# A hybrid decoder step on one core: which semaphores are cleared between stages

## The chip, the core and the metric

The kernel runs on one core of a Trainium2 chip. The metric is the device time of one execution in microseconds (us), as a median over runs. Five engines work side by side, each on its own list of instructions: TensorE (PE, with its weight loads PEld), VectorE (DVE), ScalarE (ACT), GpSimd (POOL) and SyncE (SP), which here issues most DMAs. They wait for each other only through semaphores, numbered counters that an instruction raises when it is done and another waits on.

## The reference

One decoder layer, on 512 prompt tokens and 8 x 4 sample tokens, model width 1024, all in float32:

```python
h  = x @ w_in
a  = sliding-window attention(rope(q), rope(k), v, sinks)
b  = gated delta rule(silu(conv(qkv)), beta, g), gated RMS norm
x1 = layer_norm(ALPHA * x  + concat(a, b) @ w_o)
x2 = layer_norm(ALPHA * x1 + cross_attention(x1, memory K/V))
x3 = layer_norm(ALPHA * x2 + peer(x2))
```

`peer` scores 128 + 128 keys for each of 8 heads, picks 16 of 128 x 128 experts, and sums gate x gelu(x . u) x v over them. Outputs are x3 and the new caches and states. What is computed is not touched by the change; it concerns only how the stages are kept apart.

## The kernel before

The program is a row of nine stages, each a Python function that writes the instruction lists of all five engines: `phase_project` (h and the convolution), `phase_window` (window attention, and K/V of the memory), `phase_delta` (the delta rule), `phase_mix` (empty), `phase_cross` (w_o, layer norm, cross attention, layer norm), `phase_scores` (the search keys), `phase_hidden` (the u half of the experts), `phase_combine` (the v half and the last norm) and `phase_finish` (empty). Inside a stage the order of each engine's work is written out by hand, and every dependence is a semaphore with a fixed count; the two long stages, hidden and combine, have hardware loops, whose waits are on a register's value. Every stage with work is one `nc.Block`, at whose end all engines meet.

There are two ways to get a semaphore. `c.shared_sem(name)` (L3214) takes one that is held until the whole program is written, and is never cleared by the kernel. `c.sem(name)` (L3204) takes one and notes it in the list `own` of the stage. `run_phases` (L3200) sets up that list, calls the stage, and then:

```python
        nc.clear_and_free_semaphores(own)     # L3207
        nc.all_engine_barrier()               # L3208
```

L3207 sets the stage's semaphores to zero and gives their numbers back, so that the next stage can take them again from zero. It makes instructions on GpSimd alone: for each range of neighbouring numbers one DRAIN and one range clear (in the order's listing the clear is an `ISA` row). With an empty list it makes none. L3208 makes on each engine a DRAIN and a wait for the common release, which GpSimd gives when all have come. It stays for all nine stages.

Before the change, project, window, scores, hidden and combine take nearly all their semaphores from `c.sem`, through `s = c.sem` in the last three (L2267, L2491, L2929). So do delta (L1019), cross (L1621, L1651) and the class `LayerNorm` (L1531), of which both objects, ln1 and ln2, are made in `phase_cross` (L1643, L1644). A few are shared from the start because a load or a result reaches over a stage's end, as `mem_in` (L294), `delta_states_stored` (L1038), `first_u_in` (L2272) or `hidden_stored` (L2493). Steps of one engine on itself are counted in `dve_step` and `act_step` (L3216, L3217), shared too.

Of the kernel before, what the change touches and what calls it, by code (L numbers as in the profile page):

```python
# [27 lines left out]
NT = 5  # L28
# [110 lines left out]
def words(c, at, *shape, rows=P):  # L139

    n = 1
    for s in shape:
        n *= s
    start = max(x for x in c.tensors if x <= at)
    v = c.tensors[start][0:rows, at - start:at - start + n]
    return shaped(v, *shape)
# [9 lines left out]
def cst(c, at, n, rows=P):  # L156
    return c.tensors[0][0:rows, A_CST + at:A_CST + at + n]
# [63 lines left out]
W_RING = 3  # L221
# [41 lines left out]
def phase_project(c):  # L263
# [21 lines left out]
    conv_group = {item[2]: g for g, item in enumerate(plan) if item[0] == "conv" and item[3] == 1}  # L285
    state_group, XG = next(g for g, item in enumerate(plan) if item[0] == "state"), 2 * NT

    ident_in, consts_in, x_in, state_in = c.sem("ident_in"), c.sem("consts_in"), [c.sem(f"x_in{n}") for n in range(NT)], c.sem("conv_state_in")
    piece_in = [c.sem(f"w_in_piece{s}") for s in range(W_RING)]
    w_hi, w_lo, x_lo = c.sem("w_in_high_set"), c.sem("w_in_low_set"), c.sem("proj_x_low_set")  # L290
    group_done, evacuated = c.sem("proj_group_done"), c.sem("proj_evacuated")
    pads, conv_done, sil_done = c.sem("conv_pads_set"), c.sem("conv_chunk_done"), c.sem("conv_silu_done")
    newc_set, rotated = c.sem("new_conv_rows_set"), c.sem("tile_rotated")
    c.mem_in, c.mem_w_in = c.shared_sem("mem_in"), [c.shared_sem(f"mem_weight_in{i}") for i in range(3)]  # L294

    def piece(store, p):
# [233 lines left out]
def phase_window(c):  # L530
# [20 lines left out]
    w_meml = [rounded(c, f"mem_weight_low{i}", a, KD, XD) for i, a in enumerate(W_RAW)]  # L551
    w_memh = [rounded(c, f"mem_weight_high{i}", a, KD, XD) for i, a in enumerate(W_HIGH)]
    mem_in, mem_w_in = c.mem_in, c.mem_w_in
    mem_turned, mem_hi, mem_lo, mem_done, mem_out = (c.sem("mem_" + x) for x in ("turned", "high_set", "low_set", "projected", "projected_out"))
    w_hi, w_lo = c.sem("mem_weight_high_set"), c.sem("mem_weight_low_set")
    mem_stored = [c.sem(f"mem_stored{i}") for i in range(4)]

    hd = words(c, A_HD, NT, 520)
    ss, beta, dg, dtz, alog, dtb = row_scales(c)
    squared = words(c, W_NCO, D)  # L560
    params_in, nco_stored = c.sem("delta_params_in"), c.sem("new_conv_rows_stored")
    small_act, small_dve = c.sem("row_scales_by_act"), c.sem("row_scales_by_dve")

    sink_in, sink_rows_in, keys_in, values_in = c.sem("sinks_in"), c.sem("sink_rows_in"), c.sem("window_cache_keys_in"), c.sem("window_cache_values_in")
    turned, q_out, late_turned, late_out = c.sem("q_turned"), c.sem("q_turned_out"), c.sem("late_turned"), c.sem("late_turned_out")
    scored, masked, expd, ptd, pt_out, av_done, av_out = (
        c.sem(x) for x in ("scores_done", "scores_masked", "exp_done", "probs_turned", "probs_turned_out", "window_av_done",
                           "window_av_out"))
    qm_set, masked_s, divided_s = c.sem("sample_q_set"), c.sem("sample_scores_masked"), c.sem("sample_probs_set")
    stored = c.sem("window_stored")  # L570
    units = [(n, kv) for n in range(4) for kv in range(2)]
    nu = len(units)

# [1686 lines left out]
def phase_scores(c):  # L2260
# [3 lines left out]
    q, key, keyt = words(c, F_Q, 2, 2, QW), c.keys, words(c, F_KEY + 2 * NK, 2, NK)  # L2264
    sc = words(c, F_SC, NT, 16, NK)
    ident = cst(c, K_ID, P)
    s = c.sem  # L2267
    w_in = [s(f"w_pq_in{h}") for h in range(4)]
    keys_turned, keys_out = s("keys_turned"), s("keys_turned_out")
    x_hi, x_lo, w_hi, w_lo = s("x2_high_set"), s("x2_low_set"), s("w_pq_high_set"), s("w_pq_low_set")  # L2270
    q_done, q_out, scored, score_out = s("peer_q_done"), s("peer_q_out"), s("peer_scored"), s("peer_scores_out")
# [193 lines left out]
def phase_hidden(c):  # L2465
# [22 lines left out]
    eid, head_sum, gates_of = small[:, 0:PAIRS], small[:, PAIRS:PAIRS + PH], {4: small[:, 256:384], GT: small[:, 384:512]}  # L2488
    ids, hid_s = words(c, P_IDS, ROWSETS).bitcast(U32), words(c, P_HID, ROWSETS)

    s = c.sem  # L2491
    u_in, gates_stored = ([s(f"{x}{i}") for i in range(2)] for x in ("expert_u_in", "gates_stored"))
    hid_stored = c.hid_stored = [c.shared_sem(f"hidden_stored{i}") for i in range(2)]  # L2493
    c.first_v, c.first_gated = c.shared_sem("first_expert_v_in"), c.shared_sem("first_gates_in")
# [5 lines left out]
    turned, ut_kept, ut_low, hid_done, gelu_done = (s("expert_" + x) for x in ("u_turned", "u_kept", "u_low_set", "hidden_done", "gelu_done"))  # L2500
# [413 lines left out]
def phase_combine(c):  # L2914
# [11 lines left out]
    gain, bias = cst(c, K_SWA, D), words(c, O_BIAS, D)  # L2926
    stats, mean, root, eps = words(c, O_ST, NT, 12), words(c, O_ST + NT * 12, NT, 2), words(c, O_ST + NT * 14, NT), words(c, O_ST + NT * 15, 1)
    ident = cst(c, K_ID, P)
    s = c.sem  # L2929
    g_in, h_in = ([s(f"{x}_in{i}") for i in range(2)] for x in ("gates", "hidden"))  # L2930
    v_in = [[s(f"expert_v_in{i}{e}") for e in range(2)] for i in range(2)]
    v_hi, v_lo, gated_set, g_hi, g_lo, out_done, tile_out = (s("expert_" + x) for x in (
# [1 line left out]
    x_hi, x_lo, x_added, one_set, eps_set = (s(x) for x in ("x3_high_set", "x3_low_set", "x3_added", "identity_rounded", "eps_set"))  # L2934
    row_in, row_used = [s(f"value_row_in{i}") for i in range(V_RING)], s("value_row_used")
    norm_in, quads_added = s("last_gain_and_bias_in"), s("sample_quads_added")
    var_set, std_set, y_set, stored = (s("last_" + x) for x in ("variance_set", "deviation_set", "half_tile_set", "y_stored"))
# [273 lines left out]
def hymba_step(nc, dram):  # L3211
    with ExitStack() as ctx:
# [18 lines left out]
        with ExitStack() as layer:  # L3231
            memory(layer, "layer", A_FREE, ARENA)
            run_phases(c, (phase_project, phase_window, phase_delta, phase_mix, phase_cross))
        with ExitStack() as search:
            c.xr = high_low(search, "x2_high_low", 2 * KD * TOK)
            memory(search, "scores", F_SC, F_SC_END)
            with ExitStack() as queries:
                c.wr = high_low(queries, "w_pq_high_low", 4 * KD * 2 * NK)
                memory(queries, "queries", F_SC_END, F_END)
                run_phases(c, (phase_scores,))  # L3240
            with ExitStack() as experts:
                c.utr = high_low(experts, "u_high_low", 4 * D)
                c.hot = high_low(experts, "one_hots", 2 * 3 * 4 * P)
                c.gate_hi = high_low(experts, "gates_high", TOK)
                memory(experts, "experts", F_SC_END, H_END)
                run_phases(c, (phase_hidden,))
        with ExitStack() as outputs:
            c.vr = high_low(outputs, "v_high_low", 4 * GB * D)
            c.gr = high_low(outputs, "gated_high_low", 4 * GB * TOK)
            memory(outputs, "outputs", A_FREE, O_END)  # L3250
            run_phases(c, (phase_combine,))
# [23 lines left out]
```

## Time and profile before

| | us |
|---|---|
| median of 3 runs | 2130.9 |
| lowest and highest run | 2126.84 and 2132.81 |
| the profiled execution | 2129.74 |
| its span, first to last instruction | 2127.9 |
| stage project | 0 to 174.5 |
| window | 174.5 to 282.5 |
| delta | 282.5 to 437.7 |
| cross | 437.7 to 699.9 |
| scores | 699.9 to 818.5 |
| hidden | 818.5 to 1564.3 |
| combine | 1564.3 to 2127.9 |

The stages follow each other with no overlap of their instructions. In the profile, busy time of an engine counts only its computing instructions (and GpSimd's indirect DMAs); drains, waits and semaphore clears are listed under the engine's name with a q, as POOLq, and are seen only when their line is asked for. `PEclk` is the clock granted to TensorE, 1.00 being full speed; a DMA share of 1 means that all 16 DMA engines of the core are busy.

### The profile page before, as it was taken

How to read it: one execution, taken by the hardware profiler on the slowest of the kernel's cores; microseconds unless marked ns; L12 is line 12 of the kernel's file. 1: busy time of each engine (PE TensorE's matmuls, PEld its weight loads, DVE VectorE, ACT ScalarE, POOL GpSimd, SP SyncE). 2: the span in 40 equal slices, each digit the busy share in tenths (PEclk: the TensorE clock that was granted, in tenths of full speed). 3: DMA queues.
4: the chain of work that ended last, by engine and by line, in shares of the span. 5: the costliest groups of instructions: out<-in, count | busy, mean ns of one | idle time of the engine just before them, and what ended most of it. 6: DMA issues, size and time to landing. Idle time of an engine off the chain costs nothing. (4 is left out here: it accounts for less than half of the span.)

```text
span 2127.9 us, 33947 instructions
## 1 busy us (share of the span) xinstructions
PE 2032.2 (96%) x12943; PEld 1856.7 (87%) x12943; DVE 1620.7 (76%) x3030; ACT 792.9 (37%) x1311; POOL 536.1 (25%) x334
## 2 busy tenths in 40 slices
PE   7999989889999899999999999999989999999998
PEld 7998879878856899999999999999978787787786
DVE  5735756565254326999999799999969888889898
ACT  4335453342241322323244444444433333333332
POOL 0000010000000000212112055555536555665530
PEclk9999989999999999999999999999999999999999
DMA  5224210061451403677667479998899999999993
GB/s 170 80 84 130 81 52 1 21 222 40 178 198 43 159 1 105 246 250 268 230 215 268 146 281 339 344 340 338 334 363 387 386 387 387 383 383 384 380 376 112
DMA packets 223184, 483.75 MB, mean 227 GB/s; under 512 B 11983, under 2 KB 137167, under 8 KB 221414
## 3 DMA queue, kind: packets, MB, share of 16 engines
q1 hardware_dynamic: 176998, 314.56, 41.5%
q0 software_dynamic: 46080, 167.79, 21.6%
q8 instruction: 65, 1.06, 0.2%
q14 instruction: 41, 0.34, 0.0%
HBM read 423.29 MB, written 58.36 MB: 226 GB/s over the span
## 5 line engine op out<-in xcount | busy, mean ns | idle before, releaser
L2990 PE MATMUL ps<-v_high_low,gated_high_low 128*128 128x512 f32 x2304 | 534.7, 393 | 22.5 <-ACT gated_high_low L3058 18.1
L2990 PEld LDWEIGHTS ps<-v_high_low,gated_high_low 128*128 128x128 f32 x2304 | 434.1, 189 | 122.9 <-ACT v_high_low L3056 20.4
L2594 PE MATMUL ps<-x_high_low,u_high_low 128*128 128x384 f32 x1024 | 356.4, 348 | 0.0
L2595 PE MATMUL ps<-x_high_low,u_high_low 128*128 128x384 f32 x1024 | 345.6, 337 | 0.0
L3082 POOL DMA_INDIRECT outputs<-peer_v,kept x138 | 245.5, 1779 | 180.8 <-DVE kept L3099 148.1
L2711 POOL DMA_INDIRECT scores<-peer_u,kept x64 | 93.9, 1468 | 732.5 <-DVE kept L2831 555.4
L2669 ACT ACTIVATE kept<-ps 128x384 f32<-128x384 f32 x128 | 62.9, 491 | 405.6 <-PE ps L2599 399.2
L2599 PE MATMUL ps<-x_high_low,u_high_low 128*128 128x384 f32 x1024 | 204.7, 341 | 0.0
L2595 PEld LDWEIGHTS ps<-x_high_low,u_high_low 128*128 128x128 f32 x1024 | 193.4, 189 | 0.0
L2594 PEld LDWEIGHTS ps<-x_high_low,u_high_low 128*128 128x128 f32 x1024 | 193.0, 188 | 0.0
L3162 DVE TENSOR_TENSOR v_high_low<-raw_v,v_high_low 128x1024 fp32r<-128x1024 f32 x120 | 146.2, 1218 | 53.4 <-ACT v_high_low L3056 53.4
L2599 PEld LDWEIGHTS ps<-x_high_low,u_high_low 128*128 128x128 f32 x1024 | 178.4, 188 | 0.0
L3099 DVE SCALAR_TENSOR_TENSOR kept<-outputs,kept 128x1024 f32<-128x1024 f32 x136 | 174.0, 1279 | 4.7 <-DMA outputs<-peer_v,kept 0.9
L2724 DVE TENSOR_TENSOR u_high_low<-ps,u_high_low 128x1024 fp32r<-128x1024 f32 x128 | 156.1, 1219 | 27.7 <-ACT u_high_low L2660 27.1
L3056 ACT CAST v_high_low<-raw_v 128x1024 fp32r<-128x1024 f32 x120 | 125.9, 1049 | 104.2 <-DMA raw_v<-peer_v 102.8
L3058 ACT CAST gated_high_low<-outputs 128x384 fp32r<-128x384 f32 x128 | 65.7, 513 | 240.5 <-DVE outputs L3156 237.2
L2660 ACT CAST u_high_low<-ps 128x1024 fp32r<-128x1024 f32 x128 | 133.6, 1044 | 37.4 <-PE ps L2585 33.0
L2711 POOL DMA_INDIRECT experts<-peer_u,kept x64 | 93.1, 1455 | 151.0 <-DVE experts L2732 144.0
L2585 PE MATMUL ps<-kept,experts 128*128 128x128 f32 x1008 | 130.6, 273 | 0.0
L2585 PEld LDWEIGHTS ps<-kept,experts 128*128 128x128 f32 x1008 | 116.4, 141 | 3.0 <-issue 0.2
L2680 ACT COPY scores<-ps 128x512 f32<-128x512 f32 x96 | 97.8, 1133 | 0.0
L1520 POOL TENSOR_TENSOR layer<-layer,kept 128x512 f32<-128x512 f32 (+1 forms) x5 | 6.0, 1191 | 308.1 <-DVE layer L1415 308.1
(471 smaller groups left out, 4144.8 us busy)
## 6 DMA issues: line engine op xcount, KB each, us to landing
experts<-peer_u SPq DMA_DIRECT2D x63, 1024.0 KB
raw_v<-peer_v SPq DMA_DIRECT2D x60, 1024.0 KB
hidden<-kept SPq DMA_DIRECT2D x64, 384.0 KB
gates<-scores SPq DMA_DIRECT2D x12, 2048.0 KB
first_hidden<-hidden SPq DMA_DIRECT2D x16, 768.0 KB, 17.9
outputs<-gates SPq DMA_DIRECT2D x16, 768.0 KB
outputs<-hidden SPq DMA_DIRECT2D x16, 768.0 KB
first_gates<-gates SPq DMA_DIRECT2D x15, 768.0 KB
```

Source lines behind the costliest of these rows:

```text
L2585: ins = pe.transpose(bank(c, 4 * b, D)[:, P * k:P * k + P], block_u[:, P * k:P * k + P], ident)
L2594: pe.matmul(o, utr[:, b, HI, k], xr[:, HI, k, 0:DN], start=(k == 0), stop=False)
L2595: pe.matmul(o, utr[:, b, HI, k], xr[:, LO, k, 0:DN], start=False, stop=False)
L2599: ins = pe.matmul(o, utr[:, b, LO, k], xr[:, HI, k, 0:DN], start=False, stop=(k == KD - 1))
L2660: act.copy(utr[:, b, HI], bank(c, 4 * b, D).rearrange("p (k a) -> p k a", k=KD)).then_inc(ut_kept, 1)
L2711: pool.indirect_dma_start(out=ring[i], out_offset=None, in_=d.peer_u[0], in_offset=bass.IndirectOffsetOnAxis(ap=ids[:, no:no + 1], axis=0) ...
L2724: v.tensor_tensor(utr[:, n % 2, LO], bank(c, 4 * (n % 2), D).rearrange("p (k a) -> p k a", k=KD), plain(utr[:, n % 2, HI]), ALU.subtract). ...
L2990: ins = pe.matmul(bank(c, 2 * t + h), gr[:, slot, x, DN * b + P * t:DN * b + P * t + P], vr[:, slot, y, D * b + 512 * h:D * b + 512 * h + ...
L3056: act.copy(vr[:, slot, HI, D * b:D * b + D], raw).then_inc(v_hi, 1)
L3082: pool.indirect_dma_start(out=ring[i], out_offset=None, in_=d.peer_v[0], in_offset=bass.IndirectOffsetOnAxis(ap=ids[:, no:no + 1], axis=0) ...
L3099: ins = v.scalar_tensor_tensor(into, row, g, into, ALU.mult, ALU.add)
L3162: v.tensor_tensor(vr[:, slot, LO, D * b:D * b + D], raw, plain(vr[:, slot, HI, D * b:D * b + D]), ALU.subtract).then_inc(v_lo, 1)
```

## The change

In project, window, scores, hidden and combine every `c.sem` becomes `c.shared_sem`. These semaphores are no longer in `own`, so L3207 does not clear them, and their numbers are not used again; each later stage takes numbers of its own. L3207, L3208, `LayerNorm`, `phase_delta` and `phase_cross` are as before. In words the change is that the semaphores of five stages and of both layer norms live to the program's end, and only those of the delta rule and of cross attention are cleared between stages; of the layer norms, the diff has nothing.

```diff
-    ident_in, consts_in, x_in, state_in = c.sem("ident_in"), c.sem("consts_in"), [c.sem(f"x_in{n}") for n in range(NT)], c.sem("conv_state_in")
+    ident_in, consts_in, x_in, state_in = c.shared_sem("ident_in"), c.shared_sem("consts_in"), [c.shared_sem(f"x_in{n}") for n in range(NT)], c.shared_sem("conv_state_in")
...
-    newc_set, rotated = c.sem("new_conv_rows_set"), c.sem("tile_rotated")
+    newc_set, rotated = c.shared_sem("new_conv_rows_set"), c.shared_sem("tile_rotated")
...
@@ phase_window
-    params_in, nco_stored = c.sem("delta_params_in"), c.sem("new_conv_rows_stored")
+    params_in, nco_stored = c.shared_sem("delta_params_in"), c.shared_sem("new_conv_rows_stored")
...
-    stored = c.sem("window_stored")
+    stored = c.shared_sem("window_stored")
...
@@ phase_scores, phase_hidden, phase_combine (one line in each)
-    s = c.sem
+    s = c.shared_sem
```

What it moves is seen on GpSimd. Its list from the program's start to the end of the cross and scores stages (`L1514` opens its part of delta, `L2703` its part of hidden; rows with - are of before, with + of the change):

```order
 L3263 MEMSET const-bfloat16-1.0 128x1
 L3263 MEMSET const-uint8-127 128x1
-L3207 ISA x3
 L1514 UNCONDITIONAL_BRANCH
 L1520 ISA
...
 L1522 TENSOR_TENSOR layer<-kept,layer 32x128
 L1050 UNCONDITIONAL_BRANCH
-L3207 ISA x9
+L3207 ISA x5
 L2703 UNCONDITIONAL_BRANCH
```

The three clears after project and window are gone, and of the nine after delta, cross and scores five are left. The same list from the end of hidden (`L2517`) through combine (`L3073` opens it) to the end of the program:

```order
 L2711 DMA kept<-peer_u,kept 128x1024
 L2517 UNCONDITIONAL_BRANCH
-L3207 ISA x5
 L3073 UNCONDITIONAL_BRANCH
 L3082 DMA outputs<-peer_v,kept 128x1024 x3
...
 L2954 UNCONDITIONAL_BRANCH
-L3207 ISA x5
```

Both groups of five are gone. On the other four engines every instruction keeps its place; only the numbers of the semaphores that they raise and wait on differ.

## Rows read from the trace of the kernel before

**Rows 1.** the page, part 4: the chain that ended last, share of the span by line
```profile
DMA raw_v<-peer_v 7%; SPq L2968 4%; DVE kept L3099 4%; PE ps L2990 2%; DVE v_high_low L3162 2%; DVE outputs L3156 1%; DMA outputs<-gates 1%; ACT v_high_low L3056 1%; DMA outputs<-peer_v,kept 1%; SPq L2966 0%; DVE gated_high_low L3167 0%; PE
```

**Rows 2.** stretches: start:end us, length, busy us of each engine, PEclk, DMA share, GB/s
```profile
818.50:1564.30 745.80, 739.15 (x4875) 735.52 (x4875) 705.60 (x1682) 300.77 (x375) 234.03 (x160) 1.00 0.76 275
1564.30:2127.90 563.60, 538.73 (x2320) 436.74 (x2320) 489.46 (x586) 195.01 (x266) 290.07 (x160) 0.98 0.97 357
```

**Rows 3.** instructions of L3207 over the span: ns min/median/max, first to last start
```profile
L3207 POOLq DRAIN  x22: 42/68/98, 174.2 to 2127.0; - x22
L3207 POOLq EVENT_SEMAPHORE_RANGE_CLEAR  x22: 45/80/175, 174.3 to 2127.1; - x22
```

**Rows 4.** instructions of L3207, then of L3208, from 436 to 439 us
```profile
L3207 POOLq DRAIN  x3: 53/77/95, 436.7 to 437.3; - x3
...
L3208 POOLq DRAIN  x2: 40/40/40, 437.5 to 437.7; - x2
L3208 PEldq EVENT_SEMAPHORE  x2: 51/51/51, 437.7 to 438.0; - x2
```

**Rows 5.** the same two lines, from 173 to 175.5, then 281 to 284 us
```profile
L3207 POOLq DRAIN  x1: 98/98/98, 174.2 to 174.2; - x1
...
L3208 PEldq EVENT_SEMAPHORE  x1: 51/51/51, 174.7 to 174.7; - x1
...
L3207 POOLq DRAIN  x2: 70/79/88, 281.9 to 282.2; - x2
...
L3208 PEldq EVENT_SEMAPHORE  x1: 51/51/51, 282.7 to 282.7; - x1
```

**Rows 6.** the same, from 698.5 to 701, 817 to 820, 1563 to 1566 us
```profile
L3207 POOLq DRAIN  x4: 67/86/95, 698.7 to 699.4; - x4
...
L3208 PEldq EVENT_SEMAPHORE  x1: 51/51/51, 700.0 to 700.0; - x1
...
L3207 POOLq DRAIN  x2: 49/60/71, 817.5 to 817.7; - x2
L3207 POOLq EVENT_SEMAPHORE_RANGE_CLEAR  x2: 45/68/92, 817.6 to 818.1; - x2
...
L3208 PEldq EVENT_SEMAPHORE  x1: 51/51/51, 818.5 to 818.5; - x1
...
L3207 POOLq DRAIN  x5: 42/58/81, 1563.2 to 1563.8; - x5
...
L3208 PEldq EVENT_SEMAPHORE  x1: 51/51/51, 1564.3 to 1564.3; - x1
```

**Rows 7.** the same, from 2126 to 2128 us (combine and the empty last stage)
```profile
L3207 POOLq DRAIN  x5: 55/58/87, 2126.4 to 2127.0; - x5
...
L3208 PEldq EVENT_SEMAPHORE  x2: 51/51/51, 2127.5 to 2127.9; - x2
```

**Rows 8.** stretches around boundaries, columns as in rows 2
```profile
173.00:175.50 2.50, 1.18 (x12) 0.93 (x9) 0.02 (x1) 1.09 (x2) 0.00 (x0) 1.00 0.00 0
436.00:439.00 3.00, 0.86 (x4) 0.89 (x5) 0.39 (x1) 0.30 (x1) 0.00 (x0) 0.50 0.92 291
819.80:823.20 3.40, 3.40 (x15) 3.38 (x13) 3.37 (x14) 2.91 (x3) 0.00 (x0) 0.50 0.90 337
823.20:826.60 3.40, 3.40 (x22) 3.37 (x22) 3.40 (x22) 0.51 (x2) 0.00 (x0) 1.00 0.90 224
```

**Rows 9.** timeline: start us, us, engine, line, operation, [idle before <-releaser]
```profile
174.82 0.63 PE L634 MATMUL ps<-kept,layer 128*128 128x128 f32 x4 [1.32 <-PEq L3208]
...
818.61 2.55 PE L2585 MATMUL ps<-kept,first_u 128*128 128x128 f32 x16 [2.02 <-PEq L3208]
...
1566.09 8.74 SPq L2968 DMA_DIRECT2D outputs<-hidden  x1
```

**Rows 10.** the chain in order of time: start us, us, what
```profile
1728.46 12.56 DMA raw_v<-peer_v
...
1862.65 15.98 DMA raw_v<-peer_v
```

More of the change, by code:

```diff
@@ L286, in phase_project @@
     state_group, XG = next(g for g, item in enumerate(plan) if item[0] == "state"), 2 * NT
-    ident_in, consts_in, x_in, state_in = c.sem("ident_in"), c.sem("consts_in"), [c.sem(f"x_in{n}") for n in range(NT)], c.sem("conv_state_in")
[L289 to L292, printed above, removed]
-    newc_set, rotated = c.sem("new_conv_rows_set"), c.sem("tile_rotated")
+    ident_in, consts_in, x_in, state_in = c.shared_sem("ident_in"), c.shared_sem("consts_in"), [c.shared_sem(f"x_in{n}") for n in range(NT)], c.shared_sem("conv_state_in")
+    piece_in = [c.shared_sem(f"w_in_piece{s}") for s in range(W_RING)]
+    w_hi, w_lo, x_lo = c.shared_sem("w_in_high_set"), c.shared_sem("w_in_low_set"), c.shared_sem("proj_x_low_set")
+    group_done, evacuated = c.shared_sem("proj_group_done"), c.shared_sem("proj_evacuated")
+    pads, conv_done, sil_done = c.shared_sem("conv_pads_set"), c.shared_sem("conv_chunk_done"), c.shared_sem("conv_silu_done")
+    newc_set, rotated = c.shared_sem("new_conv_rows_set"), c.shared_sem("tile_rotated")
     c.mem_in, c.mem_w_in = c.shared_sem("mem_in"), [c.shared_sem(f"mem_weight_in{i}") for i in range(3)]
@@ L553, in phase_window @@
     mem_in, mem_w_in = c.mem_in, c.mem_w_in
-    mem_turned, mem_hi, mem_lo, mem_done, mem_out = (c.sem("mem_" + x) for x in ("turned", "high_set", "low_set", "projected", "projected_out"))
-    w_hi, w_lo = c.sem("mem_weight_high_set"), c.sem("mem_weight_low_set")
-    mem_stored = [c.sem(f"mem_stored{i}") for i in range(4)]
+    mem_turned, mem_hi, mem_lo, mem_done, mem_out = (c.shared_sem("mem_" + x) for x in ("turned", "high_set", "low_set", "projected", "projected_out"))
+    w_hi, w_lo = c.shared_sem("mem_weight_high_set"), c.shared_sem("mem_weight_low_set")
+    mem_stored = [c.shared_sem(f"mem_stored{i}") for i in range(4)]
     hd = words(c, A_HD, NT, 520)
@@ L560, in phase_window @@
     squared = words(c, W_NCO, D)
-    params_in, nco_stored = c.sem("delta_params_in"), c.sem("new_conv_rows_stored")
-    small_act, small_dve = c.sem("row_scales_by_act"), c.sem("row_scales_by_dve")
-    sink_in, sink_rows_in, keys_in, values_in = c.sem("sinks_in"), c.sem("sink_rows_in"), c.sem("window_cache_keys_in"), c.sem("window_cache_values_in")
-    turned, q_out, late_turned, late_out = c.sem("q_turned"), c.sem("q_turned_out"), c.sem("late_turned"), c.sem("late_turned_out")
+    params_in, nco_stored = c.shared_sem("delta_params_in"), c.shared_sem("new_conv_rows_stored")
+    small_act, small_dve = c.shared_sem("row_scales_by_act"), c.shared_sem("row_scales_by_dve")
+    sink_in, sink_rows_in, keys_in, values_in = c.shared_sem("sinks_in"), c.shared_sem("sink_rows_in"), c.shared_sem("window_cache_keys_in"), c.shared_sem("window_cache_values_in")
+    turned, q_out, late_turned, late_out = c.shared_sem("q_turned"), c.shared_sem("q_turned_out"), c.shared_sem("late_turned"), c.shared_sem("late_turned_out")
     scored, masked, expd, ptd, pt_out, av_done, av_out = (
-        c.sem(x) for x in ("scores_done", "scores_masked", "exp_done", "probs_turned", "probs_turned_out", "window_av_done",
+        c.shared_sem(x) for x in ("scores_done", "scores_masked", "exp_done", "probs_turned", "probs_turned_out", "window_av_done",
                            "window_av_out"))
-    qm_set, masked_s, divided_s = c.sem("sample_q_set"), c.sem("sample_scores_masked"), c.sem("sample_probs_set")
-    stored = c.sem("window_stored")
+    qm_set, masked_s, divided_s = c.shared_sem("sample_q_set"), c.shared_sem("sample_scores_masked"), c.shared_sem("sample_probs_set")
+    stored = c.shared_sem("window_stored")
     units = [(n, kv) for n in range(4) for kv in range(2)]
@@ L2489, in phase_hidden @@
     ids, hid_s = words(c, P_IDS, ROWSETS).bitcast(U32), words(c, P_HID, ROWSETS)
-    s = c.sem
+    s = c.shared_sem
     u_in, gates_stored = ([s(f"{x}{i}") for i in range(2)] for x in ("expert_u_in", "gates_stored"))
@@ L2928, in phase_combine @@
     ident = cst(c, K_ID, P)
-    s = c.sem
+    s = c.shared_sem
     g_in, h_in = ([s(f"{x}_in{i}") for i in range(2)] for x in ("gates", "hidden"))
```

## The prediction

> **What bounds the kernel now.** I read the page first. Of the span of 2127.9 us, the chain that ended last runs through the loads of `peer_v`, VectorE and SyncE's queue in the last long stage [rows 1]. Nothing in these rows names a semaphore clear. Then the table by stage: the expert stage is filled by TensorE (739.15 of 745.8 us), the combining stage by its transfers (DMA share 0.97) [rows 2]. The change touches neither, so the question is only what stands between the stages. For that I asked for the instructions of L3207, the call that clears: 22 pairs of a DRAIN and a range clear, all on GpSimd, medians 68 and 80 ns [rows 3]. They are not counted as busy, so the engine table says nothing of them. What they cost must be read from the other engines: how long after a stage's end they are let go.
>
> **How a boundary runs.** At the end of a stage, all engines meet once (the Block's own barrier). Then GpSimd clears; the four others go straight to the barrier of L3208 and stand there. GpSimd joins only after its last clear, and then releases all. Nothing hides the clears, because every engine is stopped. The cost of a boundary is thus from GpSimd's first DRAIN of L3207 to TensorE's EVENT_SEMAPHORE of L3208. The program has one boundary without any clear, that of the empty `phase_mix`: there GpSimd's DRAIN of L3208 is at 437.7 and TensorE's release at 438.0, so a bare barrier takes 0.3 us [rows 4]. That is what remains where all clears go.
>
> **The sum, boundary by boundary.** Starts are printed to 0.1 us, so each difference may be off by as much, and the sum by some 0.3.
> - After project: 174.2 to 174.7 is 0.5 us with one pair, less 0.3: **0.2 us** goes [rows 5].
> - After window: 281.9 to 282.7 is 0.8 with two pairs: **0.5** [rows 5].
> - After delta: 436.7 to 437.7 is 1.0 with three pairs, so a pair costs (1.0 - 0.3)/3 = 0.23 [rows 4]. Its semaphores are still cleared. The order on GpSimd shows 9 clears of delta, cross and scores becoming 5, and scores keeps none. So 7 of delta and cross become 5: shared semaphores no longer lie scattered between the cleared numbers, and there are fewer ranges. I put one pair to each of the two stages: **0.2** here.
> - After cross: 698.7 to 700.0 is 1.3 with four pairs, a pair 0.25: **0.3** [rows 6].
> - After scores: 817.5 to 818.5 is 1.0 with two pairs: **0.7** [rows 6].
> - After hidden: 1563.2 to 1564.3 is 1.1 with five: **0.8** [rows 6].
> - After combine: 2126.4 to 2127.5 is 1.1 with five: **0.8** [rows 7]. This one is at the very end of the program, where nothing can take it back.
>
> That makes 3.5 us for 17 pairs removed, 0.2 us each. The other engines' instruction counts do not change; the waits on their instructions carry other semaphore numbers, which I cost at nothing, since the same events release them: 0.1 us after TensorE is released at 174.7 it runs its first matmul [rows 5, 9], whatever the number is called.
>
> The price of a pair has two bounds. The cheapest is the marginal pair at the end, 0.8/5 = 0.16 us, which gives 17 x 0.16 = 2.7. The dearest are the two after scores, 0.7/2 = 0.35, which gives 6.0. I take the sum by boundaries, 3.5, since each term has its own row. As a further floor only the 0.8 us at the end is kept, if each earlier stage waited for something that does not move with it.
>
> One term is doubtful. After scores, the second DRAIN takes at most 71 ns from 817.7 and its clear begins only at 818.1 [rows 6]: some 0.4 us in which GpSimd runs nothing. I count it as gained. If the gap belongs to the place in the instruction stream and not to the clear, it appears at another GpSimd instruction, and the gain is 3.1. The Trainium skill, Runtime: NRT & Kernel Launch, Instruction fetch mechanics, says that an engine's instructions come in blocks by the engine's own queue, and that crossing a block is mostly but not wholly hidden; by that rule the gap stays in the program and the sum is 3.1. No row here shows which instruction a block begins with. The same page (The launch sequence) has the runtime zero the user semaphores around the kernel whatever the kernel leaves in them; by that, the time outside the span does not grow. The profiled execution took 2129.74 us with a span of 2127.9, so 1.8 us lie outside it, and I leave them as they are.
>
> **Does a gain at a boundary last?** After project TensorE starts 0.1 us behind the release, after 1.32 us of idle time; after scores it starts at 818.61, 0.1 us behind the release at 818.5, after 2.02 us of idle time, and is busy from there on [rows 5, 6, 9]. The loads and gathers of a stage are issued by SyncE and GpSimd, which are released with the rest, so they move together with the work that uses them. So I let all 3.5 us through.
>
> Against the profiled execution: 2129.74 - 3.5 = 2126.2. It lay 1.2 us under the median of the three runs shown, 2130.9; so for the median, **2130.9 - 3.5 = 2127.4 us**, 0.16% less. The three runs spread from 2126.84 to 2132.81, more than the whole effect; about 0.3% (6.4 us) is what a measurement of this kernel can tell from no change.
>
> **Rivals.**
> - *The gain is swallowed* (chance 0.1). Loads in flight over a boundary land when they land. For it: across the boundary after delta the DMA share is 0.92 from 436 to 439 us, so early weights could be the next wait. Against it: TensorE starts that stage with the release, only the 0.2 us of that boundary hangs on it, and around the boundary after project the DMA share is 0.00 [rows 8]. For more to be lost, later stages would have to wait for loads issued a stage earlier. Kept: 0.8 to 2 us, time 2129 to 2130.
> - *The clock gives more* (0.13). After scores the granted clock is 0.50 from 819.8 to 823.2, and in that time 15 matmuls run where 22 run in the next 3.4 us at 1.00 [rows 8] (0.50 and 1.00 are 1.2 and 2.4 GHz): 3.4 x (1 - 15/22) = 1.1 us lost, and it came after the idle time of 2.02 us [rows 9], which the change cuts to 1.3. Around the boundary after project, with 1.32 us of idle time, the clock stays at 1.00 [rows 8]. If the fall does not come, 1.1 us more is gained, and a second one elsewhere may shorten too (0.50 around the boundary after delta [rows 8]): 3.5 + 1.1 to 2.2, time 2125 to 2126. With a measurement a little low this reads as faster by over 0.3%.
> - *The combining stage settles worse* (0.04): slower. Its transfers fill it, and its start is crowded: SyncE's first load of `hidden` is stuck 8.74 us in issuing [rows 9]. The release comes 0.8 us earlier, and the balance of GpSimd's gathers and SyncE's loads may fall otherwise. The chain waits 12 times for `raw_v`, mostly near 12.56 us, at the longest 15.98 [rows 10]. Each one that goes from the one to the other costs 3.4 us, so one pays back the gain and three give 10.3 - 3.5 = 6.8 us more than now, slower by over 0.3%: 2137.7. Against it: all loads and gathers of the stage start from the same release, so their distances stay.
> - *The change does not do all that its words say.* They name both layer norms, but `LayerNorm` (L1531) still takes its semaphores from `c.sem`, and both are made in `phase_cross`, so they are cleared with cross. It is in my count already (7 pairs to 5, not fewer), and worth about one pair, 0.2 us.
>
> **The numbers.** The forecast has 0.73, the swallowed gain 0.1, the clock 0.13, the slower case 0.04. From the spread of the runs a fifth or so of the first and third cases together would read as faster by over 0.3%: faster 0.16, same 0.80, slower 0.04. The range: dearest pair and the clock give 6.0 + 1.1 = 7.1 us, 2123.8, and 2.3 below that for the scatter of the runs, 2121.5; at the other end 0.8 us gained is 2130.1, and the highest run lay 1.9 above its median: 2132.0. The slower case lies outside.
>
> **What would show it.** After: 5 pairs of L3207 in place of 22, two after delta and three after cross; TensorE's release 0.3 us after the first L3208 DRAIN of GpSimd at the other boundaries; the lengths of the seven stages between releases unchanged but for a us or two; no 0.50 just after the start of the expert stage, or still one; time outside the span still 1.8. I am wrong if the pairs gone do not shift the release, if a stage between two releases is several us longer or shorter, or if GpSimd's 0.4 us gap turns up where another engine waits for it.

## The result, and the profile after

| | kernel before | changed kernel |
|---|---|---|
| median | 2129.62 us (20 runs) | 2133.26 us (20 runs) |
| lowest and highest | 2125.51 to 2133.68 | 2129.56 to 2138.32 |
| ratio, 95% interval | | 1.0021 (1.0014 to 1.0029) |
| span of the profiled execution | 2127.9 | 2130.4 |

The change made the kernel slower, by 0.21% or some 4.5 us by the ratio (3.6 between the medians). That is under the 0.3% that I had called same, but the interval leaves the sign clear, and I had forecast 3.5 us less.

The clears went as counted. Of the 22 pairs on L3207 [rows 3] five are left, two after delta and three after cross. First the lines for the whole span in the changed kernel's profile, then those around delta's and cross's ends (instructions of a line: ns min/median/max, first to last start):

```profile
L3207 POOLq DRAIN  x5: 64/90/128, 432.1 to 696.7; - x5
L3207 POOLq EVENT_SEMAPHORE_RANGE_CLEAR  x5: 45/175/291, 432.3 to 696.9; - x5
```

```profile
L3207 POOLq DRAIN  x2: 64/96/128, 432.1 to 432.6; - x2
...
L3207 POOLq DRAIN  x3: 67/90/116, 696.1 to 696.7; - x3
...
L3208 PEldq EVENT_SEMAPHORE  x1: 51/51/51, 697.3 to 697.3; - x1
```

After delta the longer of the two clears that are left takes 291 ns, where the longest of before took 175 [rows 3]. I put that down to the same semaphores lying in fewer, longer ranges; no view shows how long a range is. From GpSimd's first DRAIN to the release the boundary after cross takes 696.1 to 697.3, 1.2 us, in place of 1.3 [rows 6]. The boundary after delta takes 0.9 (432.1 to 433.0) in place of 1.0 [rows 4]. The fewer ranges brought 0.1 us at each of the two, not 0.2 and 0.3.

Where nothing is cleared any more and GpSimd has done no gathers, the boundary is the bare barrier of 0.3 us. The lines of L3208 after project (GpSimd's DRAIN, TensorE's release), after window and after scores (release alone; the Blocks ended 0.3 us earlier):

```profile
L3208 POOLq DRAIN  x1: 41/41/41, 173.0 to 173.0; - x1
L3208 PEldq EVENT_SEMAPHORE  x1: 51/51/51, 173.3 to 173.3; - x1
...
L3208 PEldq EVENT_SEMAPHORE  x1: 51/51/51, 280.6 to 280.6; - x1
...
L3208 PEldq EVENT_SEMAPHORE  x1: 51/51/51, 815.6 to 815.6; - x1
```

After scores that is 0.3 for 1.0 us [rows 6], after project 0.3 for 0.5 and after window 0.3 for 0.8 [rows 5]. So far the sum holds. The loss is in the other two boundaries. L3208 after hidden, and after combine:

```profile
L3208 POOLq DRAIN  x1: 4224/4224/4224, 1559.1 to 1559.1; - x1
L3208 PEldq EVENT_SEMAPHORE  x1: 51/51/51, 1563.5 to 1563.5; - x1
...
L3208 POOLq DRAIN  x1: 4457/4457/4457, 2125.4 to 2125.4; - x1
...
L3208 PEldq EVENT_SEMAPHORE  x2: 51/51/51, 2130.0 to 2130.3; - x2
```

GpSimd's own DRAIN takes **4224 ns** after hidden and **4457 ns** after combine. In the kernel before, the same instruction took 40 ns there, behind five clears (L3208 from 1563 to 1566 us, then from 2126 to 2128, where the empty last stage has the second):

```profile
L3208 POOLq DRAIN  x1: 40/40/40, 1564.1 to 1564.1; - x1
...
L3208 POOLq DRAIN  x2: 40/40/40, 2127.3 to 2127.6; - x2
```

In the changed kernel all engines stand there until it is done: the release after hidden comes at 1563.5, 4.4 us after the DRAIN's start, instead of 1.1 us [rows 6]; that after combine 4.6 us after it, instead of 1.1 [rows 7]. These are the two stages in which GpSimd issues gathers (indirect DMAs, L2711 and L3082), 160 in each, and it had long stopped: its last gather of the combining stage starts at 2051.20, 74 us ahead of that DRAIN (timeline, as in rows 9):

```profile
2051.20 1.01 POOL L3082 DMA_INDIRECT kept<-peer_v,kept  x1 [2.30 <-DVE kept L3099]
```

The transfers had landed too. By the DMA view, the queue that carries the gathers (`software_dynamic`) has no packet from 1552.9 to the DRAIN at 1559.1, and none from 2058.2 to the one at 2125.4: the last gather was done 6 us ahead of the one DRAIN and 67 us ahead of the other.

To see whether anything else had moved, here are four of the seven stages by themselves, without the boundaries, and the sum over all seven (columns as in rows 2). Before, then after:

```profile
282.70:436.70 154.00, 132.08 (x1232) 125.57 (x1232) 103.14 (x201) 73.77 (x210) 11.76 (x10) 0.92 0.11 32
438.00:698.70 260.70, 243.41 (x1509) 188.91 (x1509) 133.82 (x188) 74.66 (x147) 0.00 (x0) 0.98 0.37 132
818.50:1563.20 744.70, 739.15 (x4875) 735.52 (x4875) 705.60 (x1682) 300.77 (x375) 234.03 (x160) 1.00 0.76 275
1564.30:2126.40 562.10, 538.73 (x2320) 436.74 (x2320) 489.46 (x586) 195.01 (x266) 290.07 (x160) 0.99 0.98 358
sum 2120.40, PE 2032.22 PEld 1856.72 DVE 1620.69 ACT 792.93 POOL 536.07; mean PE 290.32 PEld 265.25 DVE 231.53 ACT 113.28 POOL 76.58
```

```profile
280.60:432.10 151.50, 130.31 (x1232) 123.51 (x1232) 103.15 (x201) 73.83 (x210) 11.77 (x10) 0.93 0.11 33
433.30:696.10 262.80, 246.50 (x1509) 191.01 (x1509) 133.84 (x188) 75.10 (x147) 0.00 (x0) 0.97 0.37 131
815.60:1559.10 743.50, 737.83 (x4875) 734.00 (x4875) 705.54 (x1682) 300.84 (x375) 234.47 (x160) 1.00 0.77 276
1563.50:2125.40 561.90, 537.15 (x2320) 435.45 (x2320) 489.23 (x586) 194.98 (x266) 298.90 (x160) 0.99 0.98 358
sum 2117.70, PE 2031.16 PEld 1854.44 DVE 1620.43 ACT 793.88 POOL 545.34; mean PE 290.17 PEld 264.92 DVE 231.49 ACT 113.41 POOL 77.91
```

What is left of the span when the stages are taken out is 2127.9 - 2120.4 = 7.5 us before and 2130.4 - 2117.7 = 12.7 us after: **5.2 us more at the boundaries**. Without the two DRAINs (4.224 + 4.457, less the 0.08 that two short ones take) it would be 4.1 us, 3.4 less than before: that is the forecast's 3.5. The stages differ by -2.5 us (delta), +2.1 (cross), -1.2 (hidden) and -1.2 (project, from its length of 174.2 and 173.0) in these two executions, 2.7 us less in all. Such differences need no cause in the change: over the profiles below, delta alone took from 148.69 to 156.30 us.

### The profile page after: what moved, and what is told of

It reads as the page before. It is cut to its first block and busy times, and to the rows that moved or that the text cites. A ratio compares the mean times of both kernels' runs of the same rounds, so it can differ in the third digit from the quotient of the medians.

```text
span 2130.4 us, 33913 instructions
## 1 busy us (share of the span) xinstructions
PE 2031.2 (95%) x12943; PEld 1854.4 (87%) x12943; DVE 1620.4 (76%) x3030; ACT 793.9 (37%) x1311; POOL 545.3 (26%) x334
## 5 line engine op out<-in xcount | busy, mean ns | idle before, releaser
L3082 POOL DMA_INDIRECT outputs<-peer_v,kept x138 | 256.8, 1861 | 175.5 <-DVE kept L3099 139.6
L2711 POOL DMA_INDIRECT scores<-peer_u,kept x64 | 94.1, 1470 | 730.4 <-DVE kept L2831 553.6
L2711 POOL DMA_INDIRECT experts<-peer_u,kept x64 | 93.2, 1457 | 150.8 <-DVE experts L2732 143.8
```

Of the source, the lines that this page charges most:

```text
L2711: pool.indirect_dma_start(out=ring[i], out_offset=None, in_=d.peer_u[0], in_offset=bass.IndirectOffsetOnAxis(ap=ids[:, no:no + 1], axis=0) ...
L3082: pool.indirect_dma_start(out=ring[i], out_offset=None, in_=d.peer_v[0], in_offset=bass.IndirectOffsetOnAxis(ap=ids[:, no:no + 1], axis=0) ...
```

## The experiments

The question was why a DRAIN of 40 ns became one of 4.2 us, and whether that alone is the result. Theory A: the first plain DRAIN (one of a barrier) on GpSimd behind gathers costs, the DRAIN that comes with a semaphore clear does not, and it spares the one behind it. Theory B: the cost comes from semaphores left uncleared. Further ones are in the expectations. The first four kernels ran on one chip with the kernel before at a median of 2129.1 us.

### One unused semaphore, cleared after each of the two stages

```diff
         phase(c)
+        if phase in (phase_hidden, phase_combine):
+            c.sem(f"spare_{phase.__name__}")
```

> The changed kernel, but the expert stage and the combining stage each take one unused semaphore from c.sem, so that L3207 makes one DRAIN and one range clear there. In the changed kernel's profile GpSimd's DRAIN of L3208 after these two stages took 4224 and 4457 ns (it took 40 ns before). Theory A (the first plain DRAIN after gathers costs 4.2 to 4.5 us; the DRAIN of a clear does not, and settles it): both barriers take 0.5 us instead of 4.35 and 4.58, the span is 7.9 us shorter than the changed kernel's, about 2125.5 us in time, ratio 0.998 to the kernel before. Theory B (the 4 us come from the gathers' own semaphores being left uncleared): both DRAINs of L3208 stay at 4.2 to 4.5 us, time 2133, ratio 1.002. Theory C (the DRAIN of a clear only starts the work, which then must run out): the DRAIN of L3208 behind the single clear takes about 4 us, ratio 1.002.

Measured: 2124.93 us (12 runs), ratio **0.9987** (0.9977 to 0.9997), which is 0.13% faster than the kernel before. The lines of the clear (here L3209) and of the barrier (here L3210) after hidden:

```profile
L3209 POOLq DRAIN  x1: 53/53/53, 1559.9 to 1559.9; - x1
L3209 POOLq EVENT_SEMAPHORE_RANGE_CLEAR  x1: 44/44/44, 1560.0 to 1560.0; - x1
...
L3210 POOLq DRAIN  x1: 40/40/40, 1560.1 to 1560.1; - x1
L3210 PEldq EVENT_SEMAPHORE  x1: 51/51/51, 1560.3 to 1560.3; - x1
```

The clear's DRAIN after combine:

```profile
L3209 POOLq DRAIN  x1: 58/58/58, 2121.7 to 2121.7; - x1
```

One clear of one semaphore that nothing ever raised, 53 + 44 ns, and the barrier's DRAIN is 40 ns again. The boundary takes 0.4 us from the first DRAIN to the release. Theory B falls, since all the gathers' semaphores are still uncleared, and so does C: the work is not just started and waited for later. The span is 2122.4 us, 8.0 less than the changed kernel's; by the two ratios to the kernel before, the gain is 0.34%, some 7 us. The two DRAINs had taken 8.7.

### A plain DRAIN early, hidden behind the other engines

```diff
                 pool.indirect_dma_start(...).then_inc(row_in[i], 16)
+            pool.drain()
```

Behind the gather loop, in hidden and in combine.

> The changed kernel with a plain DRAIN of GpSimd right behind its last gather of the expert stage and of the combining stage, where it has more than ten us left until the stage ends. Theory A (a fixed cost of the first plain DRAIN after gathers, paid by GpSimd alone): these new DRAINs take 4 us or more each, hidden behind the other engines, and the DRAINs of L3208 take 0.04 us; the barriers take 0.25 us each, the time falls by 8.4 us to about 2125, ratio 0.998. Theory B (uncleared semaphores are looked through at every plain DRAIN): both the new DRAINs and those of L3208 take 4 us, ratio 1.002. Theory D (the DRAIN waits for transfers of the gathers still under way): the new DRAIN is as long as the last gather's transfer, and L3208's is short; but then the changed kernel's could not have been 4 us long, 13 us or more behind the last gather.

Measured: 2125.48 us (12 runs), ratio **0.9981** (0.9971 to 0.9991). The new DRAINs in hidden and in combine, and all nine of the barriers:

```profile
L2713 POOLq DRAIN  x1: 11545/11545/11545, 1542.8 to 1542.8; - x1
...
L3085 POOLq DRAIN  x1: 10572/10572/10572, 2046.3 to 2046.3; - x1
...
L3210 POOLq DRAIN  x9: 34/40/41, 172.5 to 2120.1; - x9
```

The DRAINs take 11.5 and 10.6 us where they stand. The last transfers are still under way: the last packet of the gathers' queue lands at 1551.7 and at 2054.1, 2.6 and 2.8 us ahead of the DRAIN's end. Nobody waits for them. No barrier's DRAIN is longer than 41 ns. So a plain DRAIN spares the next one too, and what it costs depends on where it stands. Here waiting for transfers and the cost of the changed kernel are added up and can't be told apart; that a DRAIN waits for transfers alone is excluded by the changed kernel, where they had landed 6 and 67 us before.

### No barrier, or one without DRAINs, where nothing was cleared

```diff
-        nc.clear_and_free_semaphores(own)
-        nc.all_engine_barrier()
+        if own:
+            nc.clear_and_free_semaphores(own)
+            nc.all_engine_barrier()
```

> The changed kernel without L3208 where nothing was cleared (project, window, the empty mix, scores, hidden, combine, the empty finish): the meeting at the end of each Block is the only one left there. Theory A: all that these seven barriers took goes, 0.25 us five times and 4.35 and 4.58 us, together 10.2 us: time about 2123, ratio 0.997. If the 4 us are work that GpSimd owes after its gathers whatever comes next, they turn up elsewhere, at its first instruction of the combining stage (hidden there, nothing waits within 4 us but the gathers) or beyond the program's last instruction (time minus span grows from 1.8 to 6 us): ratio 1.000.

Measured: 2125.38 us (12 runs), ratio **0.9987** (0.9977 to 0.9996). And with the barrier kept, but of semaphores alone:

```diff
-        nc.all_engine_barrier()
+        nc.all_engine_barrier(sem_only=not own)
```

> The changed kernel with the barrier of L3208 kept everywhere, but made of semaphores alone, with no DRAIN on any engine, where nothing was cleared. Theory A: the two long barriers fall from 4.35 and 4.58 to 0.2 us, time 8.6 us or more less, about 2124.5, ratio 0.998. If the 4 us belong to the meeting and not to the DRAIN, they stay: ratio 1.002.

Measured: 2127.04 us (12 runs), ratio **0.9988** (0.9977 to 0.9998). The cost belongs to the DRAIN and not to the meeting, and it is not owed: with no DRAIN of GpSimd at all behind the gathers, in either kernel, the loss is gone, and the time outside the span of the profiled execution is 1.8 us in both, as before. The first of the two should have gained 2.3 us more than the kernel with the unused semaphore (10.2 against 7.9 us expected); that can't be seen in the intervals. In its profile delta took 156.30 us and combine 563.03, more than in the profiles of the kernel before, of the changed kernel and of the other three. That is one execution, the third slowest of its twelve, so it does not explain the median; where the missing gain went stays open.

### The changed kernel again

> The changed kernel once more, on the same chip as the next three and with a second profile. If the long DRAINs of L3208 belong to the program, they are there again, 4.2 and 4.5 us within 0.1, the time is near 2133 and the ratio to the kernel before near 1.002. If they were a chance of one execution, they are short and the time of the changed kernel has another cause. The lengths of the stages, which in its first profile were 2.5 us less for delta and 2.1 us more for cross than in the profile of before, show by how much they scatter.

Measured: 2135.2 us (7 runs), ratio **1.0027** (1.0016 to 1.0038) to the kernel before at 2130.8 us on this chip. All DRAINs of L3208:

```profile
L3208 POOLq DRAIN  x9: 34/40/4457, 174.3 to 2132.4; - x9
```

The longest is 4457 ns, to the nanosecond that of the first profile; the one after hidden took 4224 again. So this is no scatter of transfers or of the clock. The stages do scatter: the DRAIN after project starts at 174.3 against 173.0 us, and hidden takes 745.5 (814.0 to 1559.5) against 743.5 for the same program.

### The kernel before, with a barrier ahead of its clears

```diff
+        if phase in (phase_hidden, phase_combine):
+            nc.all_engine_barrier()
         nc.clear_and_free_semaphores(own)
         nc.all_engine_barrier()
```

> The kernel before, all its semaphores cleared as before, with one more barrier (plain DRAINs) ahead of the clears after the expert stage and after the combining stage. Theory A (the first plain DRAIN after gathers costs, whatever is cleared later): the new barriers' DRAINs take 4.2 and 4.5 us, the clears and the old barriers stay as they were; the span grows by 2 x 0.3 + 8.4 = 9 us, time about 2138, ratio 1.004. Theory B (it is the semaphores left over from earlier stages that make a DRAIN long; here none is left but the shared ones): all DRAINs short, two barriers of 0.3 us more, ratio 1.000.

Measured: 2140.01 us (7 runs), ratio **1.0044** (1.0027 to 1.0061). After hidden, the new barrier (L3208: DRAIN and release), the clears (L3209) and the old barrier (L3210), then the new one's DRAIN after combine:

```profile
L3208 POOLq DRAIN  x1: 4218/4218/4218, 1564.6 to 1564.6; - x1
L3208 PEldq EVENT_SEMAPHORE  x1: 51/51/51, 1569.0 to 1569.0; - x1
...
L3209 POOLq DRAIN  x5: 47/60/81, 1569.0 to 1569.7; - x5
...
L3210 POOLq DRAIN  x1: 40/40/40, 1569.9 to 1569.9; - x1
...
L3208 POOLq DRAIN  x1: 4465/4465/4465, 2131.7 to 2131.7; - x1
```

All semaphores are cleared as before, and yet the plain DRAIN that now comes first takes 4218 and 4465 ns. Order decides, not which semaphores live on. This is the loss of the change, brought about in the kernel before with no semaphore's life altered.

### A MEMSET of GpSimd in between

```diff
         nc.clear_and_free_semaphores(own)
+        if phase in (phase_hidden, phase_combine):
+            nc.gpsimd.memset(c.scratch[:, :], 0.0)
         nc.all_engine_barrier()
```

> The changed kernel with one small MEMSET on GpSimd (128x1) between the end of the Block and the barrier, after the expert stage and after the combining stage. If any instruction of the GpSimd engine after the gathers settles them, the DRAINs of L3208 fall to about 0.05 us. If only the DRAIN of a clear does, they stay at 4.2 and 4.5 us. If the MEMSET pays in the DRAIN's place, the release is as late as before.

Measured: 2131.7 us in a single run, which says nothing of the time; its trace is what counts here. The memset (L3209) and the barrier's DRAINs after it (L3210), after hidden and after combine:

```profile
L3209 POOL MEMSET scratch<- x2: 99/99/99, 1558.5 to 2124.8; 128x1 f32 x2
...
L3210 POOLq DRAIN  x1: 4350/4350/4350, 1558.5 to 1558.5; - x1
...
L3210 POOLq DRAIN  x1: 4584/4584/4584, 2124.8 to 2124.8; - x1
```

This compute instruction settles nothing; the DRAIN is 0.13 us longer than in the changed kernel (4350 for 4224, 4584 for 4457), about the 99 ns of the memset.

### By what the cost goes

```diff
                 pool.indirect_dma_start(...).then_inc(row_in[i], 16)
+                if no == ROWSETS // 2 - 1:
+                    pool.drain()
```

In both stages, so that 80 of the 160 gathers are left behind it.

> The changed kernel with a plain DRAIN of GpSimd in the middle of its gathers, behind half of them, in the expert stage and in the combining stage. If the cost of the first plain DRAIN is by the number of gathers since the last one, the DRAINs of L3208 halve to some 2.1 and 2.2 us; if it is fixed, they stay at 4.2 and 4.5 us and the middle ones are as long or longer, since transfers are under way there.

The DRAINs of the barrier (here L3212) after hidden and after combine:

```profile
L3212 POOLq DRAIN  x1: 6587/6587/6587, 1566.5 to 1566.5; - x1
...
L3212 POOLq DRAIN  x1: 6577/6577/6577, 2136.2 to 2136.2; - x1
```

Neither of the two expectations: fewer gathers since the last DRAIN, and the next takes *longer*, 6.58 us for 4.2 and 4.5. The single run took 2145.15 us, its span 2143.3; the middle DRAINs themselves took 16.3 and 13.5 us among running gathers. The last gathers had landed as far back as before (hidden: no packet of theirs from 1560.3 to the DRAIN at 1566.5), so 6587 ns after hidden and 6577 after combine, some 6 and 67 us behind the last landing, show that it is the number of gathers that counts and not how long ago they ended. A cost per gather that is forgotten from time to time would do this, which the next two kernels test. They move the DRAIN:

```diff
+                if no == ROWSETS - 21:
+                    pool.drain()
```

with 21 in hidden and 41 in combine for the first, 121 and 11 for the second.

> The changed kernel with a plain DRAIN of GpSimd ahead of its last 20 gathers of the expert stage and ahead of its last 40 of the combining stage. A DRAIN of L3208 took 4.2 and 4.5 us behind 160 gathers since the last plain DRAIN, and 6.6 us behind 80. Theory E (the DRAIN goes through the gathers since the last one that are still on its list, 6.58/80 = 0.082 us each; behind 160 most are off the list already, since the list is short): behind 20 it takes 1.6 us, behind 40 3.3 us. Theory F (fixed, and more where a DRAIN stood among the gathers): both take 6.6 us.

> The same with the DRAIN ahead of the last 120 gathers of the expert stage and ahead of the last 10 of the combining stage. Theory E: 0.8 us behind 10; behind 120 either up to 9.8 us, if the list holds as many, or less than 6.6, if it has been shortened on the way. Theory F: both 6.6 us.

DRAINs of L3212 after hidden and after combine, first kernel (20 and 40 gathers):

```profile
L3212 POOLq DRAIN  x1: 1687/1687/1687, 1563.9 to 1563.9; - x1
...
L3212 POOLq DRAIN  x1: 3311/3311/3311, 2127.4 to 2127.4; - x1
```

Second kernel (120 and 10 gathers):

```profile
L3212 POOLq DRAIN  x1: 952/952/952, 1561.6 to 1561.6; - x1
...
L3212 POOLq DRAIN  x1: 861/861/861, 2124.8 to 2124.8; - x1
```

Their times were 2133.09 and 2127.96 us, a single run each; the moved DRAINs themselves took from 7.8 to 11.1 us, with transfers under way. Theory F falls. In a table, gathers since the last plain DRAIN against the barrier's DRAIN:

| gathers | 10 | 20 | 40 | 80 | 120 | 160 |
|---|---|---|---|---|---|---|
| us | 0.861 | 1.687 | 3.311 | 6.58 | 0.952 | 4.218 to 4.465 |

From 10 to 80 it is a line: (6.587 - 0.861)/70 = 0.082 us for each gather, and 0.04 us besides. Behind 120, in hidden, it is what 11 cost by this line; behind 160 what 51 cost in hidden and 54 in combine. So after some 109 gathers in hidden (120 - 11 and 160 - 51) and 106 in combine GpSimd's count starts anew. That is worked out from three points, and the two of hidden lie apart by the same price, (4.224 - 0.952)/40 = 0.082 us. It fits a list of gathers which a plain DRAIN goes through one by one, finished or not, and which empties itself when it is full; the runs show the sawtooth, not the list.

## Why the prediction was wrong

- **What a boundary costs, and that nothing hides it.** Right. The bare barrier is 0.3 us in all places where the forecast used it without gathers, and all that GpSimd adds comes out in the release.
- **17 pairs less, 5 left, two after delta and three after cross.** Right. Their sum was 3.5 us; measured at the boundaries, with the two long DRAINs taken out, 3.4. With one spare clear in each of the two stages 0.13% is won (0.03 to 0.23%), 2.8 us by the ratio, which agrees with that price within a wide interval (0.6 to 4.9 us). Two terms were too large: delta's and cross's, 0.2 and 0.3 us, measured 0.1 each, since the ranges that are left take longer.
- **The step that failed** is the one that reads best: "That is what remains where all clears go", the 0.3 us taken from the boundary of the empty `phase_mix` [rows 4] and used for hidden and combine too. Mix has no gathers before it. The DRAIN of L3208 was short after hidden and combine only because five clears stood ahead of it. In the sum these two terms were gains of 0.8 us each; they are losses of 4.4 - 1.1 = 3.3 and 4.6 - 1.1 = 3.5 us. The other five, forecast at 1.9 us, measured 0.2 + 0.5 + 0.1 + 0.1 + 0.7 = 1.6: 3.3 + 3.5 - 1.6 = 5.2 us lost by starts read to 0.1 us, 5.2 by the stages taken out of the span, 4.5 in the time by the ratio. By the prediction's own sign, a release 0.3 us after the DRAIN of L3208 wherever nothing is cleared, it was wrong at these two boundaries and right at the others.
- **The rivals.** My slower rival had the wrong place (the loads of the combining stage, which took 561.9 us after 562.1) and a chance of 0.04. None of the four rivals had the mechanism: removing an instruction changes what the next one costs. The row to doubt it by was there: two boundaries of nine follow gathers, and neither was ever seen without a clear.
- **The gap of 0.4 us after scores** was gained with the clears; 0.3 us is left there. In the kernel before with a barrier more, whose program is the same up to there, it is back at the same place, the second DRAIN at most 71 ns from 819.8, its clear at 820.3:

```profile
L3209 POOLq DRAIN  x2: 49/60/71, 819.7 to 819.8; - x2
L3209 POOLq EVENT_SEMAPHORE_RANGE_CLEAR  x2: 45/68/92, 819.8 to 820.3; - x2
```

  So the gap is no chance of one execution. Whether it belongs to that pair or to the place in the instruction stream is not settled, and the DMA view speaks for the place. One of its two queues of the kind `instruction`, q14, has a transfer 0.6 to 0.7 us behind the late clear in both programs, at 818.8 us in the kernel before and at 820.9 with the barrier more. In the changed kernel q14 has none from 814 to 820 us; one comes at 821.7, 6 us into the expert stage. The view for 818 to 820, then 820 to 822 with the barrier more, then 820 to 822 in the changed kernel (packets, MB, share of 16 engines):

```profile
q14 instruction: 1, 0.01, 1.0%
...
q14 instruction: 1, 0.01, 1.7%
...
q14 instruction: 1, 0.01, 2.1%
```

  The view does not name the engine that the instructions are for; a list of GpSimd that is shorter by the removed pairs would move its transfers in this way. The doubt that I took from the Trainium skill (Runtime: NRT & Kernel Launch, Instruction fetch mechanics), by which the gap would stay in the program, is thus not answered. At the boundaries it cost nothing, since none of the changed kernel shows a gap and the 0.4 us were gained there; inside a stage no view used here would show it. That page has the runtime zero the semaphores in any case (The launch sequence); the time outside the span, 1.8 us before and after, agrees.
- **The clock.** In the changed kernel no stretch of 0.50 follows scores, as the rival asked; nor does one in the nine other profiles of kernels with the change, where TensorE is idle for 1.01 to 1.43 us there. But the kernel before with a barrier more has the full 2.02 us of idle time there and no fall either (timeline of TensorE, then stretches as in rows 2):

```profile
820.76 1.94 PE L2585 MATMUL ps<-kept,first_u 128*128 128x128 f32 x16 [2.02 <-PEq L3210]
...
819.60:823.00 3.40, 2.01 (x17) 1.80 (x17) 2.24 (x12) 1.13 (x2) 0.00 (x0) 1.00 0.34 86
823.00:826.00 3.00, 3.00 (x17) 3.00 (x18) 2.97 (x14) 2.08 (x2) 0.00 (x0) 1.00 1.05 362
```

  So of the two executions with 2.02 us of idle time one had the fall and one had not: that idle time does not bring it by itself. Whether the shorter one keeps it away stays open, and with it whether the 1.1 us are the change's to give in some executions; the medians show nothing of it.
- **The sign and the chances.** 2133.26 lies above the range's 2132.0. That it stays within 0.3% was right in letter (0.21%), but not for my reason: it is a gain of 3.4 and a loss of 8.6 us.

## What to carry to other kernels

A term that is read at one boundary may fail at another to which the engine comes in another state, here behind gathers; ask what the removed instruction did for the one behind it. Behind gathers of GpSimd, keep a semaphore clear ahead of the barrier, or put the DRAIN where GpSimd has time left, or meet by semaphores alone: each of the three made this change a gain of 0.12 to 0.19%, and they can't be told from each other. Where boundaries are the question, take the stages out of the span first; here that difference showed +5.2 us in two executions whose stages had moved 2.7 us the other way.

## What the hardware showed that I had not expected

- A barrier's DRAIN on GpSimd costs 0.082 us for each gather issued since the last plain one, whether the last landed 6 or 67 us ago (6.587 and 6.577 us behind 80), with the count starting anew after some 106 to 109: 0.861 us behind 10, 6.58 behind 80, 0.952 behind 120, 4.224 behind 160.
- The DRAIN that comes with a semaphore clear takes 53 to 58 ns at the same place and leaves 40 ns to the next. Whether it is that DRAIN or the range clear behind it that settles the gathers stays open, since no run has the one without the other. That the clear's DRAIN is itself short can't come from the range clear, which stands behind it; and a plain DRAIN at the same place takes 4.2 us. What sets the two DRAINs apart, no view shows. Why the count starts anew at 109 in hidden and at 106 in combine is open too.
- These DRAINs repeat to some ns between executions (4224 and 4224, 4457 and 4457 in the changed kernel; 4218 and 4465 in the kernel before with a barrier more), while the stages around them move by us.
